# Head matrices times Fourier weights: computed in the front of an encoder kernel, or behind the recurrent branch

## The reference, cut to what matters

```python
h = rms_norm(x, g_mix) * (1.0 + scale1) + shift1        # shift, scale, gate from c @ w_mod
z = h @ w_in                                            # u_f, u_r, u_g of 512 channels each
f = jnp.fft.fft2(u_f, axes=(1, 3), norm="ortho").real   # over the tokens and a head's 64 channels
y_f = jnp.einsum("bshd,hde->bshe", f, w_f)              # w_f: 64x64 per head
y_r = bidirectional_rglru(conv(u_r), ...) * gelu(u_g)
x = x + gate1 * (concat([y_f, y_r]) @ w_out)
```

## Time and profile before

| | |
|---|---|
| median of 3 runs | 1413.58 us (1413.54 to 1413.64) |
| the profiled execution, its own time | 1412.65 us |
| its span, first to last instruction | 1410.9 us |
| mean granted TensorE clock | 0.996 of full speed |
| PE busy | 1387.3 us, 98% |
| DVE, ACT, POOL busy | 810.6, 587.0, 472.7 us |
| share of the chain that ended last | PE 93%, issue 3%, DVE 1%, DMA 1% |

### The profile page before, as it was taken

How to read it: one execution, slowest core, us unless ns; L and a number is a source line. 1 busy time by engine, 2 the same in 40 slices (tenths; PEclk the granted TensorE clock), 3 DMA queues, 4 the chain that set the end, 5 groups by cost and what they waited for, 6 DMA issues and landing times.

```text
span 1410.9 us, 18616 instructions
## 1 busy us (share of the span) xinstructions
PE 1387.3 (98%) x7642; PEld 1186.7 (84%) x7642; DVE 810.6 (57%) x759; ACT 587.0 (42%) x701; POOL 472.7 (34%) x269
## 2 busy tenths in 40 slices
PE   5999999999999999999999999999999999999998
PEld 3777778898888888888888888888888888888887
DVE  5957688795438974555334443353665334344584
ACT  5667889665325632332222222342322223323241
POOL 0011111135003775574554545531332222332131
PEclk9999999999999999999999999999999999999999
DMA  9444321106310343343433334479997444445542
GB/s 369 166 157 166 128 80 38 45 24 200 136 60 31 112 168 120 133 150 131 164 118 116 124 146 149 161 285 388 377 381 271 150 150 155 168 171 198 200 182 90
DMA packets 75701, 231.30 MB, mean 164 GB/s; under 512 B 5729, under 2 KB 9953, under 8 KB 66786
## 3 DMA queue, kind: packets, MB, share of 16 engines
q1 hardware_dynamic: 75618, 230.12, 44.5%
HBM read 165.09 MB, written 65.01 MB: 163 GB/s over the span
## 4 chain that ended last, share of the span: by engine, by line
PE 93%; issue 3%; DVE 1%; DMA 1%; POOL 1%; SPq 1%; ACT 0%; POOLq 0%; DVEq 0%; ACTq 0%
PE bank L797 21%; PE bank L798 21%; PE bank L799 21%; PE bank L791 9%; PE bank L793 9%; PE bank L792 9%; PE bank L826 1%; DMA win_raw<-in_w_in 1%; PE bank L838 0%; DVE lo_r L2126 0%; SPq L561 0%; PE bank L816 0%; PE bank L847 0%; POOL x L2513 0%; DVE n_t L2098 0%
## 5 line engine op out<-in xcount | busy, mean ns | idle before, releaser
L797 PE MATMUL bank<-hin_hi,w_lo 128*128 128x512 f32 (+1 forms) x896 | 302.2, 337 | 0.0
L798 PE MATMUL bank<-hin_lo,w_hi 128*128 128x512 f32 (+1 forms) x896 | 301.7, 337 | 0.0
L799 PE MATMUL bank<-hin_hi,w_hi 128*128 128x512 f32 (+1 forms) x896 | 301.1, 336 | 0.0
L2244 DVE TENSOR_TENSOR hin_lo<-hin,hin_hi 128x3072 fp32r<-128x3072 f32 x28 | 138.9, 4964 | 202.4 <-ACT hin_hi L1598 202.4
L2483 POOL TENSOR_TENSOR w_lo<-w_raw,w_hi 128x2048 fp32r<-128x2048 f32 x28 | 129.6, 4629 | 327.7 <-ACT w_hi L1586 326.2
L797 PEld LDWEIGHTS bank<-hin_hi,w_lo 128*128 128x128 f32 x896 | 170.1, 190 | 18.4 <-issue 0.5
L799 PEld LDWEIGHTS bank<-hin_hi,w_hi 128*128 128x128 f32 x896 | 169.9, 190 | 18.1
L798 PEld LDWEIGHTS bank<-hin_lo,w_hi 128*128 128x128 f32 x896 | 170.1, 190 | 17.8 <-issue 0.2
L1586 ACT ACTIVATE w_hi<-w_raw 128x2048 fp32r<-128x2048 f32 x28 | 53.6, 1916 | 291.2 <-PE bank L799 184.2
L2475 POOL TENSOR_TENSOR w_lo<-w_raw,w_hi 128x512 fp32r<-128x512 f32 x43 | 65.2, 1517 | 184.3 <-ACT w_hi L1524 184.2
L1534 ACT ACTIVATE hid<-bank 128x768 f32<-128x768 f32 (+2 forms) x68 | 52.5, 773 | 163.5 <-PE bank L799 160.8
(11 more groups left out here) (289 smaller groups left out, 3161.7 us busy)
## 6 DMA issues: line engine op xcount, KB each, us to landing
hin<-hid_all SPq DMA_DIRECT2D x28, 1536.0 KB, 6.7
hid_all<-hid SPq DMA_DIRECT2D x105, 384.0 KB, 2.5
w_raw<-in_w_ff SPq DMA_DIRECT2D x36, 1024.0 KB, 9.1
mod_raw<-in_w_mod SPq DMA_DIRECT2D x16, 1024.0 KB, 5.3
w_raw<-in_w_ff SPq DMA_DIRECT2D x60, 256.0 KB, 3.4
x<-in_xT SPq DMA_DIRECT2D x5, 2048.0 KB, 14.4
w_sums<-w_raw SPq DMA_DIRECT2D x8, 1024.0 KB, 15.3
w_raw<-w_sums SPq DMA_DIRECT2D x8, 1024.0 KB, 10.3
```

Of the source, the lines that this page charges most:

```text
L797: pe.matmul(out, w_lo, v_hi, start=first, stop=False, skip_group_check=True)
L798: pe.matmul(out, w_hi, v_lo, start=False, stop=False, skip_group_check=True)
L799: return pe.matmul(out, w_hi, v_hi, start=False, stop=last, skip_group_check=True)
L2244: dve.tensor_tensor(hin_lo[n % 3][:].rearrange("p t n -> p (t n)"), hin[n % 3][:].rearrange("p t n -> p (t n)"), hin_hi[n % 3][:].rearrang ...
```

## The change

The product moves into the front of PE's stream, behind `norm_sum(1)`, in banks 2 and 4. Its two loads move up, between the loads of the first and of the second tile of w_in; dft_head was loaded there already, at the end of the front's loads, wf_raw only at j = 7. ACT copies both results to the padded buffer u_pad, which is unused until the first evacuation, SP stores them to a new tensor in DRAM (512 KB), and loads them back as a_f32 and b_f32 at j = 7. At `AB_AFTER` ACT makes the high parts from these, and DVE the low parts, so both read SBUF. ACT's order in the front changes too: mod_copy(0), root(1) and copy_rstd(0) now stand between the two splits of win_raw.

```diff
@@ SP, the front
         sp.dma_start(win_raw[:], w_in_d[TILES[0]]).then_inc(ld_win, 16)
+        sp.dma_start(dft_head[:], dft_head_d).then_inc(ld_wf, 16)
+        sp.dma_start(wf_raw[:], w_four_d).then_inc(ld_wf, 16)
         sp.dma_start(win_raw1[:], w_in_d[TILES[1]]).then_inc(ld_wg, 16)
         load_first(1)
         load_first(2)
         load_chunk(2)
         load_first(3)
-        sp.dma_start(dft_head[:], dft_head_d).then_inc(ld_dft, 16)
+        sp.wait_ge(ab_act, 2)
+        sp.dma_start(ab_d, ab_new).then_inc(st_ab, 16)
@@ SP, behind tile 7
             if j == 2 * FT - 1:
+                sp.wait_ge(st_ab, 16)
+                sp.wait_ge(mod_mm, mod_count(3 * KD - 1))
+                sp.dma_start(a_f32[:].rearrange("p f m -> p (f m)"), ab_d[:, 0]).then_inc(ld_ab, 16)
                 sp.wait_ge(wg_lo_done, FT)
-                sp.dma_start(wf_raw[:], w_four_d).then_inc(ld_wf, 16)
+                sp.dma_start(b_f32[:].rearrange("p f m -> p (f m)"), ab_d[:, 1]).then_inc(ld_ab, 16)
@@ PE
+        def head_weights():
+            pe.wait_ge(ld_wf, 32)
+            for t in range(2):
+                pe.matmul(bank[AB_BANKS[t]][:], dft_head[:, t, :], wf_raw[:], start=True, stop=True).then_inc(ab_mm, 1)
...
         norm_sum(1)
+        head_weights()
         mod_quarter_sum(0)
...
         mod_quarter(3)
+        pe.wait_ge(ab_act, 2)
         norm_sum(2)
...
-            if j == AB_AFTER:
-                pe.wait_ge(ld_dft, 16)
-                pe.wait_ge(ld_wf, 16)
-                pe.wait_ge(gate_sig, 2 * NCH * LRU_ALL)
-                for t in range(2):
-                    m = pe.matmul(bank[GB[t]][:], dft_head[:, t, :], wf_raw[:], start=True, stop=True)
-                m.then_inc(ab_mm, 1)
@@ ACT
         split_win_hi(0)
+        mod_copy(0)
+        root(1)
+        copy_rstd(0)
         split_win_hi(1)
-        root(1)
-        mod_copy(0)
-        copy_rstd(0)
+        for t in range(2):
+            act.wait_ge(ab_mm, t + 1)
+            act.activation(ab_new[:, t], bank[AB_BANKS[t]][:], ACT.Copy).then_inc(ab_act, 1)
         front_hi(0, 0)
...
+                    if j == 0 and c == 0:
+                        act.wait_ge(st_ab, 16)
...
             if j == AB_AFTER:
-                act.wait_ge(ab_mm, 1)
+                act.wait_ge(ld_ab, 32)
                 act.wait_ge(lru_ix, LRU_ALL)
-                act.activation(a_f32[:].rearrange("p f m -> p (f m)"), bank[GB[0]][:], ACT.Copy)
-                act.activation(ab_hi[:, 0].rearrange("p f m -> p (f m)"), bank[GB[0]][:], ACT.Copy)
-                act.activation(ab_hi[:, 1].rearrange("p f m -> p (f m)"), bank[GB[1]][:], ACT.Copy
-                               ).then_inc(ab_act, 1)
+                for t in range(2):
+                    m = act.activation(ab_hi[:, t], (a_f32, b_f32)[t][:], ACT.Copy)
+                m.then_inc(ab_act, 1)
@@ DVE
-        dve.wait_ge(ab_act, 1)
+        dve.wait_ge(ab_act, 3)
         for t in range(2):
-            m = dve.tensor_tensor(ab_lo[:, t].rearrange("p f m -> p (f m)"), bank[GB[t]][:],
-                                  ab_hi[:, t].rearrange("p f m -> p (f m)"), ALU.subtract)
+            m = dve.tensor_tensor(ab_lo[:, t], (a_f32, b_f32)[t][:], ab_hi[:, t], ALU.subtract)
```

More of the change, by code:

```diff
@@ L203, in build_encoder @@
     a_f32 = place("a_f32", [P, FT, P], F32, s0 + 8192)
+    assert SEQS[0] >= 2 * FT * P
+    ab_new = u_pad[:, UPAD[0] + PADL:UPAD[0] + PADL + 2 * FT * P].rearrange("p (t m) -> p t m", t=2)
     mod_row = place("mod_row", [P, CH], F32, s0 + 16384)
@@ L226, in build_encoder @@
                  for q, o in enumerate((A0, A0 + 2 * HALF, A0 + 2 * HALF + 16384, s0))]
-    wf_raw = place("wf_raw", [P, FT * P], F32, s3 + 4096)
+    wf_raw = place("wf_raw", [P, FT * P], F32, W0 + 16384)
+    b_f32 = place("b_f32", [P, FT, P], F32, s3 + 4096)
     u_f = [place("u_f0", [P, T], F32, s0 + 10240), place("u_f1", [P, T], F32, W0 + HALF),
@@ L371, in build_encoder @@
     sum_d = nc.dram_tensor("w2_sums", (2, P, NPAIR, CH), F32, kind="Internal").ap()
+    ab_d = nc.dram_tensor("ab_all", (P, 2, FT * P), F32, kind="Internal").ap()
     ps = ctx.enter_context(nc.psum_tensor("bank", [P, 8 * CH], F32))
@@ L375, in build_encoder @@
     GB, MB, NBK = (4, 5, 7), 6, 7
-    ld_vec, ld_dft, ld_win, ld_wg, ld_wf, ld_tab = map(
-        sem, ("ld_vec", "ld_dft", "ld_win", "ld_wg", "ld_wf", "ld_tab"))
+    AB_BANKS = (2, 4)
+    ld_vec, ld_wf, ld_win, ld_wg, ld_ab, ld_tab = map(
+        sem, ("ld_vec", "ld_wf", "ld_win", "ld_wg", "ld_ab", "ld_tab"))
+    st_ab = sem("st_ab")
     ld_x = [sem(f"ld_x{c}") for c in range(NCH)]
@@ L1988, in make_fold @@
                 dve.wait_ge(gate_mm, 2 * NCH * LRU_ALL)
-                dve.wait_ge(ab_mm, 1)
             u = u_f[f]
```

## The result

The changed kernel takes **1418.5 us** (median of 6 runs, 1418.08 to 1419.26) where the kernel before took 1413.68 beside it: ratio 1.0036, interval 1.0025 to 1.0046. It is 4.8 us slower. One of the six runs of the kernel before took 1533.68 us; it counts as slow and is left out of the ratio. The forecast was 1414.0, and the time lies outside its range; it is 1.2 above the 1417.3 of the second rival, the clock that falls in the new pause, which had been given 0.05. The profiled execution took 1418.93.

What follows compares the result with a forecast made beforehand. PE bounds the kernel, busy for 1387.3 of 1410.9 us. -1.71 (product) + 1.31 (wait for pq_lo) + 0.66 (lock) + 0.15 (front) = +0.4 us on 1413.58 gives 1414.0; range 1412.0 to 1414.9.

Steps and rivals of the forecast that it cites:

- the second rival: PE's new pause at 295.6 to 297.6: clock falls, dense matmuls at half speed cost 3.3 us, 1417.3; chance 0.05.
- Part 1: At 256 us: removing the product takes 1.71 us off PE; the changes on ACT and DVE count as nothing.
- Part 3: Recurrent branch's end: full DVE does not follow the 1.71; slack at pq_lo is 0.4 us, PE waits 1.3.
- Part 4: Recurrent branch: POOL's last win_lo moves to 269.06, holds yr 2.3 us and amp none; DVE 0.66 us later.
- the lock: SBUF exclusive to whichever of DVE and POOL starts first, not shared bandwidth; priced at 0.66 us on DVE near 269.
- The sum: Whole kernel: product, pq_lo wait, SBUF lock and front add to +0.4 us, 1414.0; its case had chance 0.77.
- the one at 22.3: Front: PE stood still from 22.3 to 24.2, after which the clock was 1.2 GHz for 6.7 us.
- Part 2: Front, 15 to 60 us: product fills PE's gap at 22.3; mod_first's second quarter lands at 28.3; net +0.15 us.
- its other branch: Front: if the clock stays high, mod_first's second quarter ends at 30.2, 0.9 us earlier than now.
- PE and DVE reach those with about that much to spare: Front: mod_first's third and fourth quarters and x's third chunk come 0.9 us later, with about that much slack.
- The +0.15 of the sum: Front: clock falls again, so mod_first's second quarter ends at 31.2, 0.15 us later than now.
- Rivals one and three: One: the saving is kept, 1411.0 to 1411.9, chance 0.13. Three: front product not hidden, 1415, chance 0.05.

Runs made afterwards that it cites:

- e11_short: Kernel before, product in place, with PE's third part of pq(1) waiting for the last of DVE's three low parts of pq(0) instead of the first; 1415.83 us.
- e2_cut: Kernel before with the product of head matrices and Fourier weights left out and nothing put in its place; 1417.49 us, ratio 1.0029.
- e5_order: Changed kernel with DVE's first low part of pq(0) made before the last fold instead of behind it; 1414.19 us.
- e9_cut_order: Kernel before with the product left out and DVE's first low part of pq(0) made before the last fold; 1412.29 us.
- e10_pause: Kernel before, product in place, with PE's third part of pq(1) waiting until DVE has made all three low folds of the second pair; 1419.54 us.
- e1_keep: Changed kernel with four matmuls of the old size put back at the old place behind tile 9, result unused; 1414.56 us, ratio 1.0007.
- after: The changed kernel itself, as profiled, against the kernel before; 1418.5 us, ratio 1.0036.
- e6_half: Changed kernel with half of the old product's matmuls (0.86 us) put back behind tile 9, result unused; 1414.34 us.
- e7_both: Kernel before with both early loads (384 KB) and ACT's new order in the front, product where it was; 1414.09 us.

## Why the prediction was wrong

**The medians' +4.8** can be put together so: front +1.4, product -1.8, pause +1.9, clock behind it +3.3. These terms are from the table above, from 290.81 against 290.71 less the +1.9 of the front, from 299.31, and from the 3.2 to 3.3 us lost; they add to 4.8. That it comes out so exactly is in part the choice of 1.4, a mean over five kernels, for the front, and of leaving out the 0.5 for hin_lo and the 0.4 at the end, which the profile has and the medians need not have.

**Part 1, right.** PE got 1.8 us back at 256 (forecast 1.71), and ACT's and SP's parts there cost nothing.

**Part 3 and Part 4, right in place and size.** Forecast: yr of 4 us, amp free, DVE 0.66 later by the lock, POOL at 269.1, a wait of about 2 us. Measured, with the front's 1.9 taken off: yr 3.88, amp 0.24, DVE 0.4 later, POOL at 269.0, PE 1.85 later at the third part. The lock as the Trainium skill has it in "SBUF — State Buffer", section "SBUF: two separate sides", is borne out: POOL started at 270.87, 0.13 us ahead of yr, and its 2.39 us lengthened yr by 2.12, and amp behind it not at all (0.24). PE does not keep the 1.8 it saves; the full DVE sets when it goes on.

**The second rival is the step that failed.** The sum put what the clock does behind the new pause at nothing; it was +3.2 to +3.3. The prediction priced it well, 6.7 us at half speed and 3.3 lost, and named the condition, a pause as long as the one at 22.3. By its own Parts 3 and 4, which gave a wait of about 2 us, that condition was met; the measured wait was shorter, 1.44, and the clock fell all the same, as it did behind 0.7 in e11_short. It was set aside with one sentence: "at 22.3 the work around the pause was sparse, here it is dense on both sides". e2_cut, e5_order with e9_cut_order, e10_pause and e1_keep show that density did not protect it. The sparse part of this stretch, eight matmuls of 2 columns, does not explain it either: in the changed kernel they start at 301.69, and the clock was low from 299.6. A chance of 0.05 for a mechanism whose point of decision the forecast itself reached was the error. That its 1417.3 is within 0.2 of e2_cut's 1417.49, with about the same pause and the old front, is in part luck, for in e2_cut's profile the clock was low for 10.2 us and not for 6.7.

**Part 2, half wrong.** Product at 22.5, L860 at 24.34, rc at 26.0 and L829 at 26.23 came as forecast; mod_first landed for a start at 28.87 (forecast 28.3). The clock did not fall here but stayed up, which the prediction had as its other branch (0.9 earlier, measured 0.3). What failed is the sentence on what comes behind, that "PE and DVE reach those with about that much to spare": DVE's squares of the third chunk ended at 48.06, PE stood 0.59 us for them, and 1.6 us were lost to the clock at 50. The pause that the 2.4 GHz of the front creates, by bringing PE forward, was not looked for. The +0.15 of the sum was 1.4 to 1.9.

**Rivals one and three.** The saving was kept in no run of the change. With DVE's order changed as well, e9_cut_order is 1.15 under the kernel before, but its interval (0.9983 to 1.0001) does not tell it from that, and it leaves the product out. The product was hidden as far as its own time goes.

**No version beats the kernel before.** e5_order repairs the pause, and what is left, 1.8 saved less the front's 1.4 to 1.9 and the 0.6 of the reorder, is nothing that can be told: 1414.19 against 1413.44.

## What to carry to other kernels

Before taking work off the bounding engine, find the next place where it meets a full engine, and work out the length of the pause that appears there. On PE, price that pause with what the clock does behind it: here a slip of 1.9 us cost 5.2, and elsewhere in these runs the same 1.4 us of waiting was followed by a still longer fall. If the step it waits for can be made earlier by a reorder on the other engine, do that together with the saving; if not, the "useless" work may be worth its time.

## What the runs showed that was not expected

- Behind a pause of PE of 0.7 us the granted clock went to 1.2 GHz for 3.4 us, behind 1.4 us for 6.8 us in one kernel and 10.2 us in another, behind 2.4 us for 6.8 us, and behind 0.3 us it did not, all at the same place of the program (e11_short, after, e2_cut, e10_pause, e6_half).
- The fall of 3.4 us also came with no pause at all behind eight 2-column matmuls (e7_both, clock 0.50 from 301 to 303, PE busy for 14.00 of the 14.00 us from 296 to 310).
- Where in its first 55 us the clock is low differs between profiles of nearly the same code (the table). The transposes that end it start within 0.7 us of each other in the five with the old front, and within 1.3 in the five with the new one. One profile of such a stretch cannot show what an edit did to it.
- Four unused matmuls, 1.8 us of PE, made the changed kernel 3.6 to 3.9 us faster (e1_keep).
